# Gates by indirect scatter, and the second expert layer held in eight PSUM banks

## The reference, cut to what matters

```python
q = einsum('pd,dk->pk', xb, w_q).reshape(P, 8, 2, 128)      # 8 heads, two halves
s = einsum('phcd,hcnd->phcn', q, keys)                      # 128 scores for each half
s1, i1 = top_k(s[:, :, 0], 16); s2, i2 = top_k(s[:, :, 1], 16)
cand = s1[..., :, None] + s2[..., None, :]                  # 256 sums, again the best 16
eidx = i1 * 128 + i2 at those 16;  gate = softmax(top_s)    # 8 x 16 = 128 experts a token
a = gelu(einsum('pd,ped->pe', xb, u_tab[eidx]))             # first layer
out = einsum('pe,ped->pd', gate * a, v_tab[eidx])           # second layer
```

## Time and profile before

| | |
|---|---|
| median of three runs | 2290.79 us (2287.73 to 2293.92) |
| span of the profiled execution | 2290.3 us |
| TensorE busy | 2141.3 us, 93% |
| VectorE, ScalarE, GpSimd busy | 1192.9, 852.6, 332.4 us |
| DMA | 307.25 MB, mean 134 GB/s |

### The profile page before, as it was taken

The page is one execution under the profiler, slowest core; times in us unless marked ns, Lnnn a source line. Parts: engine busy times, 40 slices in busy tenths (PEclk is TensorE's granted clock), DMA queues, the critical chain, the costliest instruction groups (busy, mean ns, idle before and its releaser), DMA issues. The chain is left out here.

```text
span 2290.3 us, 41978 instructions
## 1 busy us (share of the span) xinstructions
PE 2141.3 (93%) x16831; PEld 2044.2 (89%) x16831; DVE 1192.9 (52%) x2210; ACT 852.6 (37%) x1344; POOL 332.4 (15%) x224
## 2 busy tenths in 40 slices
PE   7999988698998989898998999999999999999996
PEld 3999548498988888888998999999999999999996
DVE  2514152611868686868536666666544444444434
ACT  2121212322277767676853222222222222222221
POOL 0400100000064646363720000000000000000000
PEclk9999978899999999999999999999999999999998
DMA  7322332221436354645566545454432343233310
GB/s 283 139 74 84 143 112 91 95 72 51 135 106 182 113 173 113 172 120 170 153 201 219 187 174 189 174 189 171 178 111 92 110 145 107 98 110 138 110 47 38
DMA packets 171165, 307.25 MB, mean 134 GB/s; under 512 B 91120, under 2 KB 91120, under 8 KB 159936
## 3 DMA queue, kind: packets, MB, share of 16 engines
q1 hardware_dynamic: 87744, 269.00, 33.7%
q10 hardware_dynamic: 82880, 34.08, 5.8%
q0 software_dynamic: 448, 2.92, 0.3%
HBM read 248.20 MB, written 57.77 MB: 134 GB/s over the span
## 5 line engine op out<-in xcount | busy, mean ns | idle before, releaser
L170 PE MATMUL ps<-hl,uh 128*128 128x260 f32 x2048 | 428.0, 290 | 18.4 <-DVE ul L1215 14.5
L1562 PE MATMUL ps<-cl,vh 128*128 128x260 f32 x2048 | 413.8, 283 | 6.4 <-DVE vl L1629 6.4
L170 PE MATMUL ps<-hh,ul 128*128 128x260 f32 x2048 | 415.3, 285 | 0.0
L170 PE MATMUL ps<-hh,uh 128*128 128x260 f32 x2048 | 414.9, 284 | 0.0
L1562 PE MATMUL ps<-ch,vl 128*128 128x260 f32 x2048 | 413.3, 283 | 0.0
L1562 PE MATMUL ps<-ch,vh 128*128 128x260 f32 x2048 | 412.6, 283 | 0.0
L170 PEld LDWEIGHTS ps<-hl,uh 128*128 128x128 f32 x2048 | 318.5, 191 | 19.6 <-DVE ul L1215 19.6
L1676 DVE TENSOR_TENSOR h<-ps,h 128x520 f32<-128x520 f32 x256 | 178.8, 698 | 301.0 <-PE ps L1562 300.9
L1562 PEld LDWEIGHTS ps<-cl,vh 128*128 128x128 f32 x2048 | 316.1, 189 | 6.7 <-issue 6.6
L170 PEld LDWEIGHTS ps<-hh,ul 128*128 128x128 f32 x2048 | 318.9, 190 | 0.0
L170 PEld LDWEIGHTS ps<-hh,uh 128*128 128x128 f32 x2048 | 318.9, 190 | 0.0
(11 more groups left out here) (179 smaller groups left out, 2643.4 us busy)
## 6 DMA issues: line engine op xcount, KB each, us to landing
us<-utab SPq DMA_DIRECT2D x128, 512.0 KB, 3.7
vblk<-vtab SPq DMA_DIRECT2D x64, 1024.0 KB, 5.2
gt<-gates_dram SPq DMA_DIRECT2D x32, 1040.0 KB, 7.4
wr<-w_ada SPq DMA_DIRECT2D x24, 1024.0 KB, 4.9
gates_dram<-stage ACTq DMA_DIRECT2D x40, 572.0 KB, 4.7
ahead_dram<-a SPq DMA_DIRECT2D x72, 260.0 KB, 2.3
aa<-ahead_dram SPq DMA_DIRECT2D x72, 260.0 KB, 5.0
wr<-w_in SPq DMA_DIRECT2D x14, 1024.0 KB, 4.8
```

The costliest lines, as they stand in the source:

```text
L170: last = nc.tensor.matmul(out[:, half, :], w[:, k, :], m[:, k, half * TH:(half + 1) * TH], start=(k == 0 and n == 0), stop=(k == KD - 1 an ...
L1562: last = nc.tensor.matmul(out[:, half, :], w, m[:, half * TH:(half + 1) * TH], start=(j == 0 and n == 0), stop=(j == GB - 1 and n == 2))
```

## The change: what it does

The gate stage and the expert stage become one stage, `peer_stage`, without loops in the program.

- First layer: all 128 blocks in one phase, each stored in `ahead_dram`. Beside blocks 0 to 79 VectorE chooses the experts of the five tiles, 16 blocks to a tile, with one subtraction of a block after every nine calls.
- Gates: no one-hot matrices. VectorE computes for each token and each of its 128 experts the address in `gates_dram`. For each of the first four tiles GpSimd issues 128 indirect DMAs, each adding 104 gates (4 bytes each) in DRAM, and waits for the landing after every 16. `gates_dram` holds 128 blocks of 128 x 416 and is cleared in the mixer stage by 16 DMAs from a tile of zeros, on SP's queue among the weight loads.
- Second layer, first 416 tokens: 128 blocks of 8 slices x 3 products, one matmul of 416 columns each, and each slice stays in its own PSUM bank over all blocks. VectorE no longer adds to an accumulator.
- The last 104 tokens (96 of the prompt and the 8 samples) get their second layer otherwise: GpSimd gathers the products of the first layer (128 indirect DMAs of 104 numbers) and the rows of v_tab (128 of 104 rows of 4 KB), and VectorE adds row times coefficient, one expert slot after the other. The sums are transposed by TensorE at the end.

```diff
-NGRP = NK // GB
-AB = 12
-AHEAD = AB * (TILES + 1)
+ND = T - TT                       # 416
+GB = 1
+AHEAD = NK
+CLEARS = 16
@@ mixer_stage, SP, behind the load of weights n
+                    c = n - ROWS_1 - 7
+                    if c == 0:
+                        sp.wait_ge(blank_ok, 1)
+                    if 0 <= c < CLEARS:
+                        size = NK // CLEARS
+                        sp.dma_start(io["gates"][c * size:(c + 1) * size]..., blank[:]...).then_inc(io["cleared"], 16)
@@ peer_stage, SP
+                def keep(m):
+                    sp.wait_ge(a_ok, m + 1)
+                    sp.dma_start(io["ahead"][m], a[:, m % NA]).then_inc(a_kept[m % NA], 16)
+                def coefficients(n):
+                    if n == 0:
+                        for i in range(TILES - 1):
+                            sp.wait_ge(scattered[i], 16 * HK)
+                    ...
+                    sp.dma_start(aa[:, n % NV], io["ahead"][n][:, 0:ND]).then_inc(aa_in[n % NV], 16)
+                    ...
+                    sp.dma_start(gt[:, n % NV], io["gates"][n]...).then_inc(g_in[n % NV], 16)
+                for m in range(1, LAST):                  # LAST = 256, LEAD = 2
+                    load(m)                               # 512 KB, waits for subtraction m - 3
+                    if 0 <= m - 6 < NK:
+                        keep(m - 6)
+                    if 0 <= m - NK + LEAD < NK:
+                        coefficients(m - NK + LEAD)
@@ peer_stage, TensorE
+                for m in range(NK):
+                    pe.wait_ge(ul_ok, m + 1)
+                    if m >= 3:
+                        pe.wait_ge(a_ok, m - 2)
+                    ...                                   # 48 matmuls of 260 columns
+                    # behind block 16i: scores of tile i, first half; behind 16i + 1: second half
+                pe.wait_ge(a_ok, NK)
+                for n in range(NK):
+                    m = NK + n
+                    pe.wait_ge(ul_ok, m + 1)
+                    pe.wait_ge(cl_ok, n + 1)
+                    for k in range(KD):
+                        for q, (w, r) in enumerate(((hi, cl), (hi, ch), (lo, ch))):
+                            last = nc.tensor.matmul(ps[:, k, 0:ND], w, r[:, n % NL, :],
+                                                    start=(n == 0 and q == 0), stop=(n == NK - 1 and q == 2))
@@ peer_stage, GpSimd
+                pool.wait_ge(io["cleared"], 16 * CLEARS)
+                for i in range(TILES - 1):
+                    pool.wait_ge(pick_ok, i + 1)
+                    for r in range(HK):
+                        if r and r % TOPK == 0:
+                            pool.wait_ge(scattered[i], 16 * r)
+                        nc.gpsimd.indirect_dma_start(
+                            out=gates, out_offset=bass.IndirectOffsetOnAxis(ap=where[:, i, r:r + 1], axis=0),
+                            in_=gate[:, i, r:r + 1], in_offset=None, compute_op=ALU.add).then_inc(scattered[i], 16)
+                pool.wait_ge(pick_ok, TILES)
+                for m in range(NK - NA, NK):
+                    pool.wait_ge(*stored(m))
+                for first in range(0, HK, GCH):           # GCH = 16, NG = 4
+                    for r in range(first, first + GCH):   # products into ag[:, r:r + 1]
+                        nc.gpsimd.indirect_dma_start(..., in_=products, ...).then_inc(ag_in[r // GCH], 16)
+                    for r in range(first, first + GCH):   # rows of v_tab into vg[:, r % NG, :]
+                        if r >= NG:
+                            pool.wait_ge(fg_ok, r - NG + 1)
+                        nc.gpsimd.indirect_dma_start(..., in_=values, ...).then_inc(vg_in[r % NG], 16)
@@ peer_stage, VectorE
+                for i in range(TILES):
+                    choose(i)                             # with low() after every nine calls
+                    while lows[0] < FIRST_LOW + A_TILE * (i + 1):
+                        low()
+                for m in range(lows[0], LAST):
+                    n = m - NK
+                    if 0 <= n + LEAD < NK:
+                        coefficients(n + LEAD)            # aa times gt, 128 x 416
+                    low()
+                    if 0 <= n + 1 < NK:
+                        low_coefficients(n + 1)
+                    while n >= 0 and sums[0] < summed(n):  # from n = 8 on, about one a block
+                        gathered()                        # fg += vg * ag[:, r], 104 x 1024
```

More of the change, by code:

```diff
@@ L144, in build @@
         io["ahead"] = ahead_dram
[L146 to L177, removed]
+        peer_stage(nc, sem, sb, pair, halves, residual, on_chip, hh, hl, qp, io)
 def mixer_stage(nc, sem, sb, pair, halves, residual, on_chip, hh, hl, qp, io, w_dram):
@@ L1014, in _, with scores @@
+                sp.wait_ge(y_out, 16 * KD // 2)
             @block.tensor
             def _(pe):
-                def scores(i):
-                    for m in range(4):
-                        pe.wait_ge(qt_ok, i * 4 + (m + 1))
-                        if m >= 2:
-                            pe.wait_ge(s_ok, i * 4 + (m - 1))
-                        elif m == BANK_T and positive(i):
-                            pe.wait_ge(pt_ok, i)
+                def scores(i, first, past):
+                    tile = slice(i * TT, (i + 1) * TT)
+                    for m in range(first, past):
+                        if i or m >= 2:
+                            pe.wait_ge(s_ok, i * 4 + m - 1)
@@ L1079, in _ @@
+                for k in range(KD):
+                    for half in range(2):
+                        last = nc.tensor.matmul(pair(1)[:, half, :], ones, squares[:, k, half * TH:(half + 1) * TH],
+                                                start=(k == 0), stop=(k == KD - 1))
+                last.then_inc(fss_mm, 1)
             @block.scalar
             def _(act):
-                tiles_of_qp = qp[:].rearrange("p j (i t) -> p i j t", t=TT)
-                chunks = io["gates"].rearrange("g p (i c) a t -> i c p g (a t)", c=TT // CH)
@@ new lines, in gelu, with scores @@
+                def gelu(m):
+                    act.wait_ge(w_mm, m + 1)
+                    if m >= NA:
+                        act.wait_ge(*stored(m - NA))
+                    nc.scalar.activation(halves(a[:, m % NA]), pair(1 + m % 3), ACT.Gelu_apprx_tanh).then_inc(a_ok, 1)
+                def scores(i, first, past):
+                    if i and first == 0:
+                        act.wait_ge(pick_ok, i)
+                    for m in range(first, past):
+                        act.wait_ge(s_mm, i * 4 + m + 1)
@@ L1261, in choose @@
+                def choose(i):
                     sets = range(2 * PH)
+                    calls[0] = 0
                     for j in sets:
```

752 lines of the change are left out of this document (246 added, 506 removed).

## The result

The changed kernel takes 2509.46 us (median of 4 runs, 2505.4 to 2513.96) beside 2291.60 us of the kernel before: 1.0952 times as long, 95% interval 1.0935 to 1.0969. The forecast was 1935 us, the range ended at 2220. Rival B is what happened, with a part of rival C behind it. The experiments e7, e9 and e11 were timed four times each, within 0.6%; the others once.

A forecast was written before the change was run, and what follows sets the result against it. TensorE's matmuls were taken as the bound: 563.8 mixer + 2 clearing + 766 first layer + 0.7 + 568.3 second layer + 5 traffic + 28.8 end = 1934.6, forecast 1935 us; 8-in-10 range 1900 to 2220.

The forecast's parts named there:

- Rival B: Slower than before: scatter queue at 1.7 us or more each outlasts the first layer; 2474 us at 2.0; chance 0.15.
- rival C: DMA bounds the second layer: 176 MB take 607 us, 39 more than TensorE needs, total 1974 us; chance 0.07.
- Step 3: Scatters of gates on GpSimd beside the first layer: 512 at 0.9 us plus 32 landings, 535 us, hidden within 642 us.
- My upper bound: Price of one indirect DMA on GpSimd from above: 0.90 plus 1.23 us for reading and scaling indices, 2.13 us.
- Rival A's lock: Scatters outlast first layer, chance 0.28; VectorE blocking GpSimd adds 0.5 us per gather, 0.4 per scatter, total 2044 us.
- Step 4: Last tile's 256 gathers in the second layer: hidden up to 1.3 us each, 7 x (17x - 22.2) beyond; nothing at 0.9.
- Step 5: DMA traffic in the second layer: 176 MB in 568 us, 310 GB/s, costing 5 us in all.
- Step 1: Second layer in eight PSUM banks: 3072 matmuls of 416 columns at 185.0 ns, 568.3 us, gain 169 us.
- Step 2: One-hot matrices gone from the gate stage: 136 us of matmuls leave TensorE; first layer takes 766 us.
- the late subtractions: First layer: VectorE's subtraction after each tile's choosing comes 3 us late, half counted, 8 us over 5 tiles.
- Clearing: Clearing 27 MB in the mixer shares SP's queue with weight loads: from nothing to 10 us, taken as 2.
- Ends: Kernel's end: 25.8 us now, about 3 more for copies, transposes and squares, 28.8; stage start stays, one barrier goes.

The follow-up runs named there:

- e7: Changed kernel with repeated gates merged on VectorE, plain scatters, 104 a tile over 128 partitions via DRAM, tiles every 25 blocks: 2144.98 us, 0.935 times the kernel before.
- e9: e7 with VectorE's first-layer subtractions placed closer together while it merges repeated gates: 2585.2 us, 1.1286 times the kernel before.
- e11: e9 with the tiles of choosing started every 24 blocks instead of 25: 2589.6 us, 1.1309 times the kernel before.
- e2: Changed kernel, one DMA kind per tile: tile 0 adding scatter, 1 plain scatter, 2 adding with 48 entries, 3 gather; gates wrong: 2365.1 us.
- e1: Changed kernel with only the first 64 of each tile's 128 scatters issued, gates of heads 4 to 7 left out: 2063.4 us.
- e13: e9 with the addition in DRAM put back on its 416 scatters: 2342.6 us.
- e8: e7 without the way through DRAM, so 128 scatters of 104 entries a tile: 2256.0 us.
- e3: Changed kernel gathering 128 of the 1024 columns of each value row, result partly wrong: second layer 659 us, span 2468.7 us.
- e6: Changed kernel with both e3's narrow row gathers and e4's interleaved product gathers: second layer 636 us, span 2452.7 us.
- e4: Changed kernel with product gathers issued one by one between row gathers after the first 16: second layer 715 us, span 2521.7 us.
- e12: e8 with the denser subtraction spacing of e9: 2710.3 us.
- e10: e9 with all 128 product gathers before the first row gather and row sums from second-layer block 32 instead of 8: 2644.0 us.

## Why the prediction was wrong

- **Step 3 failed, and decided it.** The step priced a scatter at 0.9 us, "the row with the smallest runs", with 2.3 us a landing, 535 us in all. Measured: 1098 us. The parts: the issue of a plain indirect DMA, 0.97 to 0.99 us (e2), is near what I took; the addition in DRAM is 0.6 us more (1.59 - 0.99, 307 us for 512), which no row contains, since all are plain; 0.30 us between two issues, 174.5 us with what else is idle there, which I had put at nothing, since rows of single DMAs can't show it; and VectorE beside it, 40 us. The landings came out right by luck: 69.3 us against 32 x 2.3 = 74, but the kernel has 28 waits and one costs 2.5 us. My upper bound, 2.13, held (1.89 alone and 2.01 in the mean, landings apart); the choice between ends 4 times apart by the nearest row was wrong, as the nearest row differed in the very operation. The place, the chain through SP and the hidden time were right: 659.4 us for the first scatter against 663, TensorE's stop at 1308.1 against 1305, and e1 shows that the hole is theirs alone.
- **Rival B** carried the right mechanism with 0.15, and its 456 us of hole at x = 2.0 is what came (456.4 of standstill at 2.01). That its total, 2474, is within 30 us of the span is in part luck: it has 83 us for the gathers' bursts, and the second layer's 124 us are bytes as well.
- **Rival A's lock.** Its 0.5 us per gather is what the second layer shows (1.52 and 1.35 us against 0.97 alone), its 0.4 per scatter is not: 0.08 in the mean of all, but that mean takes in the hole, where VectorE is idle; in the first layer alone it is about 0.13, in e2's first tile 0.18 and in e13 0.20. Plain ones lose 0.21 (e8) and 0.28 (e7).
- **Step 4, gathers.** x = 1.44 + 0.30 is beyond the 1.3 named, and 7 x 7.4 us would be 52. The seven stands are there, 60 us in all, so that mechanism was right; the price that I fed it, 0.9, was too low. What they are worth is less, 23 us (e3 against e6), and as long as the bytes bind, nothing (e4 was 18 us slower).
- **Step 5, traffic, failed too.** 5 us was taken and rival C had 39; the second layer takes 120 more than its 577 us of matmuls. The window moves 172 MB at 247 GB/s with the engines 92% busy, where I had scaled 357 GB/s from a window at 51%. This stage has 1.6 KB rows and gathers on a second queue, which that window had not; which of them costs the throughput was not run. Of the 120, e3 takes 38 away by bytes, e6 23 by order, and about 59 remain in e6, with GpSimd's issue at 589 us and the clock at 0.97; that rest isn't divided.
- **Step 1 right:** 188 ns against 185.0, 577 against 568. **Step 2 right:** 749.0 us for the first 126 blocks and 11.5 for two more at the same pace, 760.5 against 766; the late subtractions cost 5.8 us in five waits, where 8 were forecast. **Clearing** 0, and the mixer ends 4.7 us earlier; taken 2. **Ends** 26.6 against 28.8.

## What to carry to other kernels

Price an indirect DMA by its kind, not by the nearest plain DMA: here 0.97 us of GpSimd to gather, 0.99 to scatter, 1.6 to scatter with addition, 0.3 between two, for the plain ones hardly by the number of entries, and up to three times that beside wide VectorE work; where hundreds stand before a queue that others use, that sum is the kernel. Make the addresses unique and fill all partitions before asking DRAM to add, and then look whether TensorE still keeps its pace beside the plain scatters: e7 gained 364 us by them, e9 to e12 lost more than the addition costs. Where the bounds of a price stand on both sides of a threshold and no row has the operation itself, the nearest row is a weak reason for either side.

## What was not expected of the hardware

TensorE can be slowed by GpSimd's indirect DMAs without any semaphore between them. In e9 to e12, with plain scatters at one per 1.27 to 1.30 us in the slow stretches, it fell to one instruction per 1.4 us for 100 us and more in each of the four tiles, 412 to 529 us of issue time in all. In e2, which has the changed kernel's own order of work, it fell beside the one tile of plain scatters (58.3 us), and in e10 also beside 128 product gathers in a row (49.3 us). With adding scatters (the changed kernel, e13, tiles 0 and 2 of e2) it did not. In e7 and e8, with the same plain scatters but a TensorE that now and then waited for VectorE, it did not either.

The scatters' rate alone does not separate them: the first 24 of e7 start 1.40 us apart in the mean, and so do those of e9 up to TensorE's fall; 1.27 us is the rate once VectorE stands too. What is shared is open: the DMA engines were 2 to 7% busy in e9's slow stretches, and no instruction transfer ran in the one that I looked through (740 to 860 us of e9). That e7 keeps clear of it was measured in four runs, but not understood.

For the plain issue the Trainium skill, "DMA: Bandwidth & Descriptors", section "Latency and other measured facts", has about 1 us of emission overhead on the software path; the 0.97 and 0.99 us here agree, and the adding scatters' 1.59 us lie above it.
